# Three projections and the retention stage of a two-block network: the operand split and the order of the heads written anew

## The reference, cut to what matters

```python
def retention_scan(q, k, v, log_gamma, s0):          # chunks of 128 tokens
    def step(S, inp):
        qc, kc, vc = inp
        scores = einsum('bhid,bhjd->bhij', qc, kc) * decay_in
        out = einsum('bhij,bhjd->bhid', scores, vc) + einsum('bhid,bhde->bhie', qc * q_dec, S)
        S = S * chunk_dec + einsum('bhjd,bhje->bhde', kc * k_dec, vc)
        return S, out
# forward and backward over context and latent tokens, 8 heads of 64
q, k = axial_rope(q), axial_rope(k)
lat = silu(gf) * head_rms(y_f) + silu(gb) * head_rms(flip(y_b))
```

## Time and profile before

| | us |
|---|---|
| median of 3 runs | 5256.56 |
| lowest and highest | 5249.79, 5265.85 |
| the profiled execution, its own time | 5261.83 |
| its span in the trace | 5259.5 |
| first projection: split of the first slice to last copy-out | 126.4 to 657.3 |
| retention: first load to last `lT` | 662.3 to 956.9 |
| second projection, from its first load | 2712.1 on |
| third projection, from its first load | 3324.0 on |

### The profile page before, as it was taken

How to read it: one execution, slowest core, us unless ns; L and a number is a source line. 1 busy time by engine, 2 the same in 40 slices (tenths; PEclk the granted TensorE clock), 3 DMA queues, 4 the chain that set the end, 5 groups by cost and what they waited for, 6 DMA issues and landing times. The chain is left out here.

```text
span 5259.5 us, 73582 instructions
## 1 busy us (share of the span) xinstructions
PE 4237.6 (81%) x29457; PEld 2929.0 (56%) x29457; DVE 2475.1 (47%) x3963; ACT 1713.8 (33%) x3199; POOL 420.4 (8%) x383
## 2 busy tenths in 40 slices
PE   4799954678987766999929999687779887499995
PEld 1688843338886324676628444465644444266663
DVE  2211157565665456565542454316610134366664
ACT  2111023454553213454331243216620122144442
POOL 0000011220001100000000231000000000100001
PEclk7899977879998887999969999898989988699998
DMA  6222111463223327999742332121121222599997
GB/s 245 75 85 84 65 65 54 121 201 86 82 77 125 122 79 281 368 363 367 278 164 88 118 103 75 72 110 52 37 80 48 88 64 92 198 371 381 384 383 290
DMA packets 416672, 844.25 MB, mean 161 GB/s; under 512 B 35360, under 2 KB 236096, under 8 KB 413176
## 3 DMA queue, kind: packets, MB, share of 16 engines
q1 hardware_dynamic: 395896, 781.60, 41.3%
q0 software_dynamic: 12032, 41.96, 2.5%
q10 hardware_dynamic: 8448, 16.56, 0.9%
HBM read 675.66 MB, written 164.36 MB: 160 GB/s over the span
## 5 line engine op out<-in xcount | busy, mean ns | idle before, releaser
L397 PE MATMUL psum<-proj_hi,proj_w 128*128 128x512 f32 (+2 forms) x1728 | 460.7, 355 | 35.4 <-DVE proj_lo L463 35.4
L397 PEld LDWEIGHTS psum<-proj_hi,proj_w 128*128 128x128 f32 (+1 forms) x1728 | 305.0, 188 | 83.3 <-issue 35.6
L2530 PE MATMUL psum<-qkv_w,hT 128*128 128x512 f32 x768 | 335.4, 595 | 13.1 <-DMA qkv_w<-in_w_in 13.1
L2322 ACT ACTIVATE moe_hi<-moe_raw 128x2048 fp32r<-128x2048 f32 x128 | 245.1, 1917 | 301.7 <-PE psum L2273 248.2
L2357 DVE TENSOR_TENSOR moe_lo<-moe_raw,moe_hi 128x2048 fp32r<-128x2048 f32 x128 | 291.5, 2289 | 86.9 <-ACT moe_hi L2322 84.7
L397 PE MATMUL psum<-proj_lo,proj_w 128*128 128x512 f32 (+2 forms) x864 | 306.4, 355 | 0.0
L3898 DVE TENSOR_TENSOR moe_lo<-moe_raw,moe_hi 128x2048 fp32r<-128x2048 f32 x128 | 287.0, 2285 | 33.8 <-ACT moe_hi L3864 33.8
L2530 PEld LDWEIGHTS psum<-qkv_w,hT 128*128 128x128 f32 x768 | 145.3, 191 | 190.6 <-issue 176.2
L3864 ACT ACTIVATE moe_hi<-moe_raw 128x2048 fp32r<-128x2048 f32 x128 | 238.1, 1906 | 22.5 <-DMA moe_raw<-in_w_gate_up 22.2
L3118 PE MATMUL psum<-branches_T,mixed_w 128*128 128x512 f32 x512 | 222.5, 598 | 14.3 <-DMA mixed_w<-in_w_attn_o 14.3
L2283 PE MATMUL psum<-moe_wd,moe_hidT 128*128 128x512 f32 x512 | 224.2, 596 | 9.5 <-DVE moe_hidT L2378 9.5
(11 more groups left out here) (602 smaller groups left out, 8758.0 us busy)
## 6 DMA issues: line engine op xcount, KB each, us to landing
moe_raw<-in_w_gate_up SPq DMA_DIRECT2D x128, 1024.0 KB, 16.9
moe_raw<-in_w_gate SPq DMA_DIRECT2D x64, 1024.0 KB, 7.1
moe_raw<-in_w_up SPq DMA_DIRECT2D x64, 1024.0 KB, 7.5
moe_wd<-in_w_down SPq DMA_DIRECT2D x64, 1024.0 KB, 9.8
moe_wd<-in_w_down SPq DMA_DIRECT2D x32, 2048.0 KB, 11.6
mod_w<-in_w_mod SPq DMA_DIRECT2D x24, 1024.0 KB, 14.2
uT<-proj_out SPq DMA_DIRECT2D x35, 640.0 KB, 2.9
chunks_pr<-prim SPq DMA_DIRECT2D x40, 512.0 KB, 4.1
```

Source lines behind the costliest of these rows:

```text
L397: last = nc.tensor.matmul(bank[e * nch + c][0:width[e], 0:n], l, r, start=(k == 0 and i == 0), stop=(k == KD - 1 and i == 2))
L2322: nc.scalar.activation(hi[:, n % R], raw[:, n % R], ACT.Copy).then_inc(s["hi_ready"], 1)
L2530: last = nc.tensor.matmul(bank[2 * (n % 2) + c_][:, :], hT[:, k, i * P:(i + 1) * P], w[:, m % 2, k, c_ * BANK:(c_ + 1) * BANK], start=(k = ...
```

## The change

Two functions are replaced. In `gemm_T` the masking step and the tile `top` are gone: ScalarE copies `raw` straight into the fp32r tile (`leading`), VectorE subtracts that tile from `raw` (`rest`), for the weights and for the activations alike. `raw` has two buffers. TensorE's first 24 matmuls wait slice by slice. All groups are written out, without a hardware loop. In `retention` the four pairs are written out too, with two buffers for most tiles, and the work of the next pair (rotation, row steps, first scores, scan) stands between the outputs of this one. Each head works on its own half of the rows or columns instead of against zeros. The sums of squares go through 32-row statistics (`zsel`), whose root and reciprocal are taken on 32x128 values and spread back by matmuls (`spread`). The cosine product of the rotation moves from GpSimd to VectorE; GpSimd takes one of the two gate products. The rest of the program is the same.

```diff
-        raw, top = st.sb("raw", [P, KD, GW]), st.sb("top", [P, KD, GW])
+        raw = st.sb("raw", [P, 2, KD, GW])
...
+                def load(g):
+                    n = sum(size[g])
+                    sp.dma_start(raw[:, g % 2, :, 0:n], w[:, g * GW + col0:g * GW + col0 + n].rearrange("(k p) n -> p k n", p=P))\
+                        .then_inc(w_in[g % 2], 16)
+
+                load(0)
+                load(1)
+                for g in range(G):
+                    if g + 2 < G:
+                        sp.wait_ge(hi_ready, g + 1)
+                        sp.wait_ge(lo_ready, g + 1)
+                        load(g + 2)
...
+                                if g == 0 and e == 0 and c == 0:
+                                    pe.wait_ge(x_lo, k + 1)
...
-                pe.wait_ge(x_hi, KD)
-                pe.wait_ge(x_lo, KD)
-                with pe.Fori(0, TURNS) as it:
-                    for s in range(2):
...
-                def split(g, slot, width=GW):
-                    act.wait_ge(topped, g + 1)
-                    nc.scalar.activation(wt[:, slot, 0, :, 0:width], top[:, :, 0:width], ACT.Copy).then_inc(hi_ready, 1)
-
-                act.sem_inc(ev[0], 1)
+                def leading(g):
+                    n = sum(size[g])
+                    act.wait_ge(w_in[g % 2], 16 * (g // 2 + 1))
+                    if g >= 2:
+                        act.wait_ge(mm[1], nch * (g - 1))
+                    nc.scalar.activation(wt[:, g % 2, 0, :, 0:n], raw[:, g % 2, :, 0:n], ACT.Copy).then_inc(hi_ready, 1)
+
                 for k in range(KD):
-                    act.wait_ge(x_top, k + 1)
-                    nc.scalar.activation(hi[:, k, :], ob[:, k % 2, :], ACT.Copy).then_inc(x_hi, 1)
-                    if k < 2:
-                        split(k, k)
-                groups_of(act, 0, split)
+                    nc.scalar.activation(hi[:, k, :], actT[:, k, :], ACT.Copy).then_inc(x_hi, 1)
+                    if k == 0:
+                        leading(0)
...
+                def rest(g):
+                    n = sum(size[g])
+                    dve.wait_ge(hi_ready, g + 1)
+                    if g >= 2:
+                        dve.wait_ge(mm[1], nch * (g - 1))
+                    nc.vector.tensor_tensor(wt[:, g % 2, 1, :, 0:n], raw[:, g % 2, :, 0:n], wt[:, g % 2, 0, :, 0:n], ALU.subtract)\
                         .then_inc(lo_ready, 1)
 
-                dve.sem_inc(ev[1], 1)
                 for k in range(KD):
-                    if k >= 2:
-                        dve.wait_ge(x_hi, k - 1)
-                    leading(ob[:, k % 2, :], actT[:, k, :]).then_inc(x_top, 1)
-                    dve.wait_ge(x_top, k + 1)
-                    nc.vector.tensor_tensor(lo[:, k, :], actT[:, k, :], ob[:, k % 2, :], ALU.subtract).then_inc(x_lo, 1)
-                    if k < 2:
-                        split(k, k)
-                groups_of(dve, 1, split)
+                    dve.wait_ge(x_hi, k + 1)
+                    nc.vector.tensor_tensor(lo[:, k, :], actT[:, k, :], hi[:, k, :], ALU.subtract).then_inc(x_lo, 1)
+                    if k == 0:
+                        rest(0)
...
+        kvm = st.sb("kvm", [P, NB, 2, H])
+        S = st.sb("S", [P, 2, 2, NB, H])
...
+                def outer(p, j):
+                    pe.wait_ge(s["kfb_ready"], NB * p + j + 1)
+                    for d in range(2):
+                        for h in range(2):
+                            ins = nc.tensor.matmul(tr_bank[j % 2][half[h], 2 * P + d * H:2 * P + (d + 1) * H], kfb[:, j % 2, d, half[h]],
+                                                   vr[:, p % 2, j, half[h]], start=True, stop=True)
+                    ins.then_inc(s["kv"], 1)
...
+                def outputs(p, j):
+                    jj, a = j // 2, j % 2
+                    pe.wait_ge(s["sc_ready"], 2 * (4 * p + jj + 1))
+                    if j == 0:
+                        pe.wait_ge(s["scan"], SCAN * (p + 1))
+                        pe.wait_ge(s["q_scaled"], 2 * (p + 1))
+                    if NT * p + j >= 2:
+                        pe.wait_ge(s["y_ev"], 2 * (NT * p + j - 1))
+                    for d in range(2):
+                        for h in range(2):
+                            nc.tensor.matmul(y_bank[j % 2][half[h], d * P:(d + 1) * P], S[half[h], p % 2, d, 2 + j, :],
+                                             qs[half[h], p % 2, d, tok(j)], start=(d == 0), stop=False,
+                                             skip_group_check=True)
+                    for h in range(2):
+                        ins = nc.tensor.matmul(y_bank[j % 2][half[h], 0:2 * P], vr[:, p % 2, 2 + j, half[h]],
+                                               sc[:, jj % 2, h, a].rearrange("p d i -> p (d i)"), start=False, stop=True,
+                                               skip_group_check=True)
+                    ins.then_inc(s["y_mm"], 1)
...
+                            at = 30 - (16 * d + 2 * j)
+                            ins = nc.tensor.matmul(st_bank[0:32, 0:P], zsel[:, at:at + 32], sq[:, d, tok(j)],
+                                                   start=(j == 0 and d == 0), stop=(j == NT - 1 and d == 1))
+                    if jj == 3:
+                        ins.then_inc(s["st_mm"], 1)
+
+                def broadcast(p):
+                    pe.wait_ge(s["rs_ready"], p + 1)
+                    for n in range(4):
+                        if 4 * p + n >= 2:
+                            pe.wait_ge(s["normed"], 4 * p + n - 1)
+                        for a in range(4):
+                            ins = nc.tensor.matmul(bc_bank[n % 2][:, tok(a)], spread[0:32, 4 * n + a, :], rs[:, :], start=True, stop=True)
+                        ins.then_inc(s["bc_mm"], 1)
...
+                    for jj in range(4):
+                        if jj < 3:
+                            scores(p, jj + 1)
+                        steps = ((), (), (0, 1, 2, 3, 4), (5, 6, 7, 8, 9, 10))[jj]
+                        for a in range(2):
+                            outputs(p, 2 * jj + a)
+                            if jj == 1 and a == 0 and p + 1 < PAIRS:
+                                rotate(p + 1, 1)
+                            for i in steps[a:a + 1]:
+                                row_step(p + 1, i)
+                        if jj:
+                            stats(p, jj - 1)
+                        elif p + 1 < PAIRS:
+                            rotate(p + 1, 0)
+                        if jj == 3:
+                            stats(p, 3)
+                        for i in steps[2:]:
+                            row_step(p + 1, i)
+                    if p + 1 < PAIRS:
+                        scores(p + 1, 0)
+                    broadcast(p)
...
-                        dve.wait_ge(s["chain"], link(nc.vector.reciprocal(tmp[:, d, :], tmp[:, d, :])))
-                    for d in range(2):
-                        dve.wait_ge(s["chain"], link(nc.vector.tensor_tensor(y[:, d, :], y[:, d, :], tmp[:, d, :], ALU.mult)))
...
+                def variance(p):
+                    dve.wait_ge(s["st_mm"], p + 1)
+                    if p:
+                        dve.wait_ge(s["bc_mm"], 4 * p)
+                    nc.vector.tensor_scalar(rs[:, :], st_bank[0:32, 0:P], 1.0 / RET_DIM, EPS, ALU.mult, ALU.add).then_inc(s["ms"], 1)
+
+                def normed(p):
                     dve.wait_ge(s["root"], p + 1)
-                    for d in range(2):
-                        dve.wait_ge(s["chain"], link(nc.vector.reciprocal(tmp[:, d, :], tmp[:, d, :])))
-                    for d in range(2):
-                        dve.wait_ge(s["chain"], link(nc.vector.tensor_tensor(y[:, d, :], y[:, d, :], tmp[:, d, :], ALU.mult)))
-                    for d in range(2):
-                        dve.wait_ge(s["silu"], p * 2 + (d + 1))
-                        dve.wait_ge(s["chain"], link(nc.vector.tensor_tensor(y[:, d, :], y[:, d, :], g[:, d, :], ALU.mult)))
-                    nc.vector.tensor_tensor(lT[:, ds(p, 1), :], y[:, 0:1, :], y[:, 1:2, :], ALU.add).then_inc(s["lat_ready"], 1)
-                    link.end()
+                    nc.vector.reciprocal(rs[:, :], rs[:, :]).then_inc(s["rs_ready"], 1)
+                    dve.wait_ge(s["y_ev"], 2 * NT * (p + 1))
+                    for n in range(4):
+                        o = y[:, p % 2, n // 2, (n % 2) * BANK:(n % 2 + 1) * BANK]
+                        dve.wait_ge(s["bc_mm"], 4 * p + n + 1)
+                        nc.vector.tensor_tensor(o, o, bc_bank[n % 2][:, :], ALU.mult).then_inc(s["normed"], 1)
...
+                for p in range(PAIRS):
+                    for jj in range(4):
+                        if jj < 3:
+                            masked(p, jj + 1)
+                        if jj < 2 and p + 1 < PAIRS:
+                            rope(p + 1, jj)
+                        if jj == 1 and p:
+                            gated(p - 1)
```

(47 more changed lines are left out.)

431 lines of the change are left out of this document (207 added, 224 removed).

## The result

| | median of the runs shown | ratio to before, 95% interval | profiled execution: span | TensorE clock |
|---|---|---|---|---|
| before | 5256.56 us | 1 | 5259.5 us | 0.903 |
| after | 5139.12 us (5133.01 to 5143.49) | 0.9767 [0.9748, 0.9786] | 5131.2 us | 0.906 |

The medians differ by 117 us, the ratio with its interval stands for 112 to 132 us, the profiled spans differ by 128.3 us; forecast 137. The time lies in the forecast's own range, 20 us above its value. In what follows the granted clock of TensorE is a share of 2.4 GHz; 1.00 is its upper level and 0.50 (1.2 GHz) its lower one, and a value between them is a mean over a stretch that holds both.

What follows compares the result with a forecast made beforehand. Steady projections were taken as TensorE-bound, retention as a chain through all engines. Savings of 50.3 us in the heads and 87 in the retention made 137, from 5256.6 to 5119 us; own range 5098 to 5142.

Steps and rivals of the forecast that it cites:

- What bounds the kernel: Whole kernel: TensorE full in steady projections, so only their heads can shrink; retention is a chain with no engine full.
- The heads, 50.3 us: Starts of the three projections: earlier first copy-outs sum to 54.8 us, less 4.5, saving 50.3 us.
- may still owe the spell, I take 1.5: Each projection's head: TensorE's slow-clock spell may remain after the slices, between 0 and 2.5 us, taken as 1.5.
- The first chain: Retention's start: loads, rotations, row steps, masks and state updates, with outputs beginning at 698.3 instead of 705.13.
- The first pair, 46.5 us: Retention's first pair of heads: a steady pair's 49 us without gates, so 46.5 us.
- The steady pair, 49 us: Retention's middle turns: VectorE's order 41.4 us, plus 3.5 for GpSimd and 4 for TensorE's clock: 49 instead of 69.
- The undisturbed sum of 41.4: Steady retention pair: VectorE's operations and waits in order, before GpSimd and clock costs, take 41.4 us.
- GpSimd, 3.5 us a pair: Retention: GpSimd operations stretch VectorE's cosine products and gates; bounds 0 and 6.4 us a pair, taken as 3.5.
- The last pair, 27 us: Retention's end: the last pair has no next pair's work beside it and takes 27 us.
- TensorE becomes the bound: Rival in the retention: short waits keep TensorE's clock at 0.5, a pair costs 62 us, time 5166; chance 0.25.
- all overlaps: Rival: added costs hide, a retention pair costs 41.4 us and heads gain 55, time 5090; chance 0.17.
- written-out code starved nothing: Rival in the projections: fetching written-out matmuls at 0.28 us each loses 219 us, time 5338; chance 0.04.

Runs made afterwards that it cites:

- e1: The kernel before with only the new `gemm_T`, `retention` left as it was: 5198.33 us, ratio 0.9884 to before.
- e2: The kernel before with only the new `retention`, `gemm_T` left as it was: 5196.64 us, ratio 0.9879 to before.
- e7_best: Changed kernel with outer products in their own PSUM bank, GpSimd's q scaling after k's rotation, and six unread products before broadcasts: 5091.06 us, ratio 0.9683 to before.
- the bank alone: Changed kernel with the row steps' outer products in a PSUM bank of their own: 5114.17 us, ratio 0.9723 to before.
- e9_filler3: Changed kernel with three unread TensorE products before the broadcasts of each pair but the last: 5126.69 us, ratio 0.9755 to before.
- e6_filler: Changed kernel with six unread TensorE products before the broadcasts of each pair but the last: 5123.85 us, ratio 0.9745 to before.
- e5_pool_late: Changed kernel with GpSimd's scaling of q put off until VectorE has rotated k: 5111.62 us, ratio 0.9724 to before.

## Why the prediction held, and where it was off

- *What bounds the kernel.* Right. Nothing changed in the steady part of the projections, and both touched stages counted with their full length; e1 and e2 add up.
- *The heads, 50.3 us.* Right in mechanism, small in size: 56.6. The term "may still owe the spell, I take 1.5" was zero, since the clock rose by 139.9 in the slices' pace; that is 4.5 of the 6.3 us. The subtractions came 1.41 and 1.15 us apart, not 1.49 and 1.23 (1.7 us in all), and the last three products ran at the upper level (1.3 us); the weights of the second projection came 6.1 us after their issue instead of 5.0, which took 1.1 back.
- *The first chain.* Forecast 36.0 us from the first load to the outputs; TensorE's first output was at 684.36, 41.3 us. The mis-sized terms: the row step at 1.25 us was 1.75, and with the first two steps running together the row steps took 16.4 us (662.42 to 678.83) where 12.5 stood; the two collisions of 2.53 and 2.23 us had no term here, and the rotations took 10.7 us (651.80 to 662.50) instead of 8.3. Masks and scan together were 1 us shorter than put (the scan 3.2 us, not 4.8). With both causes removed (e7_best), the first output's copy comes 7.5 us earlier than in the changed kernel.
- *The first pair, 46.5 us.* From its first output to that of the next it took 48.3 (684.36 to 732.70).
- *The steady pair, 49 us.* 53.5 and 55.0. The term that was mis-sized is again the row steps: 10 us and 2 for the work between stood in the sum, and from the first to the last `ret_kfb` they took 18.4 (752.37 to 770.81). That excess of 6.4 is as large as the whole miss of 4.5 and 6.0. The 18.4 shrank to 14.1 by the bank alone, to 15.6 by GpSimd alone (744.22 to 759.85), hardly by the fillers (17.7), and to 12.6 by all three (735.46 to 748.03). Of the 7.5 us that stood for collisions and the clock the rows show 4.8: 2.4, and in the broadcasts 1.7 us for each of four products where 1.1 stood. With these the sum is 52.6; the last 1 to 2 us of the turn were not traced. The undisturbed sum of 41.4 was good: e7_best turns in 41.7 and 44.8.
- *GpSimd, 3.5 us a pair.* The mechanism holds. Directly it cost 2.4 a pair (9.6 in all), but taking it away gave 15 to 19; where the rest comes from was not separated. The cosine products for q had no GpSimd operation beside them and stayed at 681 ns, so the full 6.4 a pair did not come. The Trainium skill, SBUF — State Buffer, section "SBUF: two separate sides", states that a two-input VectorE operation and a reading GpSimd operation exclude each other; the 2.53 beside 5.09 us and the 684 ns without it agree.
- *The last pair, 27 us.* 25.7.
- *Rivals.* "TensorE becomes the bound" (62 a pair) and "all overlaps" (41.4) were both wrong as a whole, and the truth lay between at 54; three more edits bring the turn near the all-overlaps sum. The shorter head did come, and written-out code starved nothing: 521 products in 100 us as before. That the loop should have cost something did not follow from the rule quoted there, which speaks of branches out of the fetched window only; nothing here shows that this loop's branch was one.

Errors of both signs, +6 in the heads and −17 in the retention, leave 127 of the 137 us, and the spans differ by 128. In the retention the miss is 5.3 us in the first chain, 1.8 in the first pair, 4.5 and 6.0 in the steady pairs, and 0.9 the other way in the last. That the heads gave more than put was luck for the total: the retention alone was off by a fifth.

## What to carry to other kernels

When a stage is a chain through all engines, sum its undisturbed steps first; here that sum lay 0.3 and 3.4 us under the turns that three more edits reached, and most of what was above it went with them. Before pricing a chained step, list every semaphore that its first instruction waits for and ask which of them is only there because two results share a bank. A short wait of TensorE can cost twice, as the wait and at the lower clock behind it: covering 5.4 us of waiting in three turns (16 us) returned 20 to 24 in the stage, and filling half of it returned nothing that could be measured. What an upstream delay costs need not be its own length: removing 9.6 us returned 15 to 19.

## What the runs showed of the hardware

- After 13 us of idling TensorE went from 0.63 to 0.39 us for a product of 512 columns 3.5 us after its start, although it worked only in the pace of the slices. In the other two projections it took 5 and 6 us (changed kernel, 2633.02 and 3225.80).
- In waits of a few microseconds it fell again: behind a wait of 5.50 or 2.73 us the same 32 broadcast passes took 7.19 us (832.90 in the changed kernel, 727.69 in e9_filler3), behind one of 0.15 us 4.05 (e6_filler, 723.48). Behind one of 1.92 us they took 4.98 (e9_filler3, 782.79).
- GpSimd and VectorE both on SBUF: 1884 against 684 ns for the same product in the mean of eight, and GpSimd's two halves took 5.09 us beside it, 4.66 alone (e5_pool_late at 659.03).
